# Forgetting attention: scores and running sums in two float32r products over all 128 rows

## What is computed

```python
log_f = jax.nn.log_sigmoid((f_logit + f_bias).astype(jnp.float32))
cum = jnp.transpose(jnp.cumsum(log_f, axis=1), (0, 2, 1))
scale = HEAD_DIM ** -0.5
outs = []
for i in range(s // FOX_BLOCK):                      # 4 blocks of 128 queries
    start, end = i * FOX_BLOCK, (i + 1) * FOX_BLOCK
    sc = jnp.einsum('bqhd,bkhd->bhqk', q[:, start:end], k[:, :end]) * scale
    sc = sc + cum[:, :, start:end, None] - cum[:, :, None, :end]
    causal = (start + jnp.arange(FOX_BLOCK))[:, None] >= jnp.arange(end)[None, :]
    sc = jnp.where(causal[None, None], sc, -jnp.inf)
    probs = jax.nn.softmax(sc, axis=-1).astype(v.dtype)
    outs.append(jnp.einsum('bhqk,bkhd->bqhd', probs, v[:, :end]))
out = jnp.concatenate(outs, axis=1).reshape(b, s, 1024) * jax.nn.silu(z)
```

## Time and profile before

| | |
|---|---|
| median of three runs | 3423.32 us (3422.49 to 3426.72) |
| span of the profiled execution | 3422.6 us |
| TensorE busy | 3340.3 us, 98% |
| GpSimd busy | 2116.8 us, 62% |
| VectorE busy | 1552.0 us, 45% |
| ScalarE busy | 878.8 us, 26% |

### The profile page before, as it was taken

One profiled execution on the slowest core, in us unless ns is written; L12 is line 12 of the kernel. 1 busy time (PEld: TensorE's weight loads), 2 busy tenths in 40 slices (PEclk: granted clock), 3 DMA queues, 4 the chain that ended last, 5 costly groups with the idle time before them and its releaser, 6 DMA issues.

```text
span 3422.6 us, 49035 instructions
## 1 busy us (share of the span) xinstructions
PE 3340.3 (98%) x16926; PEld 2712.7 (79%) x16926; DVE 1552.0 (45%) x2835; ACT 878.8 (26%) x1851; POOL 2116.8 (62%) x2084
## 2 busy tenths in 40 slices
PE   8999999999999999999999999999999999999997
PEld 6778788887777788887888778787878877788876
DVE  6544542106545541107674652333476656423325
ACT  2133211102133211103332540323132335313321
POOL 7745577767745577766557557454856566564455
PEclk9999999999999999999999999999999999999998
DMA  3212122222211222222222222112222222221111
GB/s 136 86 62 74 64 97 98 98 98 87 86 62 62 73 99 98 94 94 98 72 86 85 76 74 94 67 62 74 87 78 85 74 99 74 75 86 68 69 71 66
DMA packets 40030, 281.42 MB, mean 82 GB/s; under 512 B 4832, under 2 KB 5344, under 8 KB 6464
## 3 DMA queue, kind: packets, MB, share of 16 engines
q1 hardware_dynamic: 38880, 277.96, 22.8%
q10 hardware_dynamic: 992, 1.31, 0.1%
HBM read 277.16 MB, written 2.10 MB: 82 GB/s over the span
## 4 chain that ended last, share of the span: by engine, by line
PE 87%; DVE 7%; issue 3%; ACT 2%; POOL 1%; DMA 0%; DVEq 0%; ACTq 0%; SPq 0%; POOLq 0%
PE banks L380 21%; PE banks L382 20%; PE banks L381 20%; PE banks L639 2%; PE banks L640 2%; PE banks L641 2%; PE banks L423 2%; PE banks L424 2%; PE banks L425 2%; PE banks L915 1%; PE banks L939 1%; PE banks L926 1%; PE banks L610 1%; PE banks L918 1%; PE banks L857 1%
## 5 line engine op out<-in xcount | busy, mean ns | idle before, releaser
L343 POOL TENSOR_SCALAR whi<-raw 128x512 fp32r<-128x512 f32 x1040 | 725.9, 707 | 1271.5 <-PE banks L382 1037.4
L348 POOL TENSOR_TENSOR wlo<-raw,whi 128x512 fp32r<-128x512 f32 x1040 | 1435.7, 1391 | 0.0
L380 PE MATMUL banks<-xhi,whi 128*128 128x512 f32 x2832 | 1136.2, 401 | 30.4 <-POOL wlo L348 20.2
L382 PE MATMUL banks<-xhi,wlo 128*128 128x512 f32 x2832 | 1107.1, 391 | 0.0
L381 PE MATMUL banks<-xlo,whi 128*128 128x512 f32 x2832 | 1106.1, 391 | 0.0
L380 PEld LDWEIGHTS banks<-xhi,whi 128*128 128x128 f32 x2832 | 533.6, 188 | 163.7 <-issue 47.2
L381 PEld LDWEIGHTS banks<-xlo,whi 128*128 128x128 f32 x2832 | 533.9, 189 | 114.8 <-issue 8.2
L382 PEld LDWEIGHTS banks<-xhi,wlo 128*128 128x128 f32 x2832 | 533.2, 188 | 113.9
L380 PE MATMUL banks<-yhi,whi 128*128 128x512 f32 x544 | 214.7, 395 | 10.1 <-POOL wlo L348 5.2
L382 PE MATMUL banks<-yhi,wlo 128*128 128x512 f32 x544 | 211.8, 389 | 0.0
L381 PE MATMUL banks<-ylo,whi 128*128 128x512 f32 x544 | 211.8, 389 | 0.0
(11 more groups left out here) (277 smaller groups left out, 4197.6 us busy)
## 6 DMA issues: line engine op xcount, KB each, us to landing
raw<-weights SPq DMA_DIRECT2D x260, 1024.0 KB, 4.8
x<-x_in SPq DMA_DIRECT2D x4, 512.0 KB, 8.0
out<-merged SPq DMA_DIRECT2D x1, 2048.0 KB, 6.3
rot<-const SPq DMA_DIRECT2D x1, 512.0 KB, 11.7
rot<-const ACTq DMA_DIRECT2D x1, 512.0 KB, 3.7
wide_mask<-const ACTq DMA_DIRECT2D x1, 384.0 KB, 4.5
wide_mask<-const SPq DMA_DIRECT2D x1, 256.0 KB, 12.0
cst<-const SPq DMA_DIRECT2D x1, 232.0 KB, 9.3
```

Source lines behind the costliest of these rows:

```text
L343: pool.tensor_scalar(whi[p][:, w], raw[p][:, w], 1.0, 1.0, ALU.mult, ALU.mult).then_inc(s("hi_written"), 1)
L348: return pool.tensor_tensor(wlo[p][:, w], raw[p][:, w], whi[p][:, w].bitcast(F32), ALU.subtract)
L380: pe.matmul(dst, whi[p][:, w], hi[:, k, :], start=start and i == 0, stop=False)
L382: mm = pe.matmul(dst, wlo[p][:, w], hi[:, k, :], start=False, stop=stop and last_k)
```

## The change

The queries and keys of a pair of heads now come from one wave (q of the pair in one tile, k of the pair in the other), and are kept as four float32r tiles of 128 rows for each head h, `part[h]`, named by what they hold. With o the 64 rows of the head and z the other 64:

- Q_HL: rows o the high part of q, rows z its low part
- Q_HS: rows o the high part of q, rows z the selector column of the head, spread over 512 columns
- K_HH: the high part of k in both
- K_LC: rows o the low part of k, rows z the running sums

So Q_HL x K_HH + Q_HS x K_LC is high x high + low x high + high x low + the running sums. Two sets of these tiles alternate between pairs. ScalarE writes the high parts and the selectors (`pair_high`), VectorE the low parts (`pair_low`), in which it subtracts the high part from the PSUM bank; the sums are written to K_LC once a layer. `fox_pick` is no longer called in the loop. There are still 20 waves, in another order: the first pair and v of group 0 ahead of the loop, and two waves behind step 31. On ScalarE half_out moves behind the exponentials of the next step; on VectorE the work on a half wave (`half_low`) comes last in a step.

```diff
+def fox_kind(w):
+    g, i = divmod(w, 4)
+    if w >= 14:
+        return "gate", w - 14
+    return (("pair", 2 * g + 1), ("z", g), ("pair", 2 * g + 2), ("v", g + 1))[i]
...
-        fox_q = (sg[:, 0:4, :], q2)
-        fox_v = (sg[:, 4:6, :].rearrange("p a n -> p (a n)").rearrange("p (c n) -> p c n", c=QB), v2)
+        fox_pair = ((fox_even[:, 0], fox_even[:, 1]), (fox_odd0[:, :, :], fox_odd1[:, :, :]))
+        Q_HL, Q_HS, K_HH, K_LC = range(4)
+        fox_v = (v_even[:, :, :], v2[:, :, :])
...
-                wave_t(fox, 0, xhi, xlo, first_bank=0)
-                wave_t(fox + 1, 1, xhi, xlo, first_bank=4)
-                start_wave(fox + 2, 0)
-                wave_s_blocks(0, range(QB)).then_inc(wave_done, 1)
+                wave_t(fox, 0, xhi, xlo)
+                start_wave(fox + 1, 1)
+                wave_s_blocks(1, range(QB)).then_inc(wave_done, 1)
...
                 def fox_scores(k):
-                    g, m = divmod(k, PAIRS)
-                    if m == 0:
-                        pe.wait_ge(drained[1], fox + 4 * g + 4)
-                        pe.wait_ge(drained[0], fox + 4 * g + 4)
-                        pe.wait_ge(s("fox_ready"), L * GROUPS + g + 1)
+                    pair, i = divmod(k, QB)
+                    if i == 0:
+                        pe.wait_ge(s("fox_split"), 2 * (2 * GROUPS * L + pair + 1))
                     if k:
                         pe.wait_ge(s("fox_probs"), 2 * STEPS * L + 2 * k)
-                    r, i = fox_unit(2 * k)
                     w = (i + 1) * P
-                    q = fox_q[g % 2]
+                    part = fox_pair[pair % 2]
                     for h in range(2):
-                        o = 64 * h
-                        pe.matmul(psum[:, 4 + h, 0:w], q[o:o + 64, r // 2, i * P:w],
-                                  q[o:o + 64, 2 + r // 2, 0:w], start=True, stop=False)
-                    for h in range(2):
-                        pe.matmul(psum[:, 4 + h, 0:w], sel[:, r + h, :], cum[:, 1, 0:w],
+                        pe.matmul(psum[:, 4 + h, 0:w], part[h][:, Q_HL, i * P:w], part[h][:, K_HH, 0:w], start=True, stop=False)
+                        pe.matmul(psum[:, 4 + h, 0:w], part[h][:, Q_HS, i * P:w], part[h][:, K_LC, 0:w],
                                   start=False, stop=True).then_inc(s("fox_scores"), 1)
...
-                half_wave(4 * GROUPS, 0, False)
+                half_wave(4 * GROUPS, 0)
                 fox_output(STEPS - 1)
-                half_wave(4 * GROUPS, 1, False)
+                half_wave(4 * GROUPS, 1)
+                for half in range(2):
+                    half_wave(4 * GROUPS + 1, half)
...
+                def pair_high(pair, keys, src):
+                    part = fox_pair[pair % 2]
+                    if pair >= 2 and not keys:
+                        act.wait_ge(s("fox_scores"), 2 * STEPS * L + 8 * (pair - 1))
+                    own.begin()
+                    for h in range(2):
+                        o, z = slice(64 * h, 64 * h + 64), slice(64 - 64 * h, 128 - 64 * h)
+                        if keys:
+                            own(act.activation(part[h][o, K_HH, :], src[o, :], ACT.Copy))
+                            own(act.activation(part[h][z, K_HH, :], src[o, :], ACT.Copy))
+                        else:
+                            own(act.activation(part[h][o, Q_HL:Q_HS + 1, :], src[o, None, :].to_broadcast([64, 2, S]), ACT.Copy))
+                            c = C_SEL + 2 * pair + h
+                            own(act.activation(part[h][z, Q_HS, :], cst[z, c:c + 1].to_broadcast([64, S]), ACT.Copy))
+                    own.done()
+                    act.nop().then_inc(s("fox_high"), 1)
...
                 for k in range(STEPS):
                     g, m = divmod(k, PAIRS)
-                    half_out(fox_wave(g, m), m % 2)
                     fox_turned_out(2 * k)
                     fox_turned_out(2 * k + 1)
                     if k + 1 < STEPS:
                         fox_expo(2 * k + 2)
                         fox_expo(2 * k + 3)
+                    half_out(fox_wave(g, m), m % 2)
                     if m == 0 and g:
                         fox_y_hi(g - 1)
...
+                def pair_low(pair, keys, src, p):
+                    part = fox_pair[pair % 2]
+                    dve.wait_ge(s("fox_high"), 2 * (2 * GROUPS * L + pair) + keys + 1)
+                    own.begin()
+                    for h in range(2):
+                        o, z = slice(64 * h, 64 * h + 64), slice(64 - 64 * h, 128 - 64 * h)
+                        to, high = (part[h][o, K_LC, :], K_HH) if keys else (part[h][z, Q_HL, :], Q_HL)
+                        own(dve.tensor_tensor(to, src[o, :], part[h][o, high, :].bitcast(F32), ALU.subtract))
+                    own.done()
+                    dve.nop().then_inc(s("fox_split"), 1)
+                    dve.nop().then_inc(drained[p], 1)
...
-                fox_pick(0)
+                for part in fox_pair:
+                    for h, z in ((0, slice(64, 128)), (1, slice(0, 64))):
+                        own(dve.tensor_copy(part[h][z, K_LC, :], cum[0:64, 1, :].bitcast(F32)))
+                own.done()
+                pair_low(0, 0, bank(0), 0)
+                pair_low(0, 1, bank(1), 0)
...
-                    if m == PAIRS - 2 and g < GROUPS - 1:
-                        fox_pick(g + 1)
+                    half_low(fox_wave(g, m), m % 2)
```

More of the change, by code:

```diff
@@ L205, in program @@
         merged = sb("merged", [P, KT, S], F32, big)
+        over_sg = ExitStack()
+        fox_even = sb("fox_even", [P, 2, 4, S], F32R, over_sg)
+        over_sg.close()
         sg = sb("sg", [P, KT, S], F32, big)
@@ L225, in program @@
         second = ExitStack()
+        over_kv = ExitStack()
+        v_even = sb("v_even", [P, QB, 256], F32, over_kv)
+        over_kv.close()
         kv_first = sb("kv_first", [P, S], F32, second)
+        sel = sb("sel", [P, 4, P], F32R, second)
         cum = sb("cum", [P, 2, S], F32R, second)
-        sel = sb("sel", [P, 4, P], F32R, second)
         selp = sb("selp", [P, 2 * P], F32R, second)
@@ L243, in program @@
         t4 = ExitStack()
+        over_q2 = ExitStack()
+        fox_odd0 = sb("fox_odd0", [P, 4, S], F32R, over_q2)
+        over_q2.close()
         q2 = sb("q2", [P, 4, S], F32, t4)
@@ L250, in program @@
         st2 = sb("st2", [P, 4, 32], F32, t4)
+        over_q3 = ExitStack()
+        fox_odd1 = sb("fox_odd1", [P, 4, S], F32R, over_q3)
+        over_q3.close()
         q3 = sb("q3", [P, 3, S], F32, t4)
@@ L934, in fox_output @@
                         pe.wait_ge(s("fox_read"), L * GROUPS + g + 1)
-                        pe.wait_ge(drained[0], fox + 4 * g + 6)
+                        pe.wait_ge(drained[1], fox + 4 * g + 4)
                     pe.wait_ge(s("fox_pt"), 2 * STEPS * L + 2 * k + 2)
@@ L942, in fox_output, with half_wave @@
                     mm.then_inc(s("fox_outputs"), 1)
-                def half_wave(w, half, tokens):
-                    n, p = fox + 3 + w, (w + 1) % 2
+                def half_wave(w, half):
+                    n, p = fox + 2 + w, w % 2
                     if half == 0:
@@ L950, in half_wave @@
                     pe.wait_ge(drained[1 - p], n + p + half + 1)
-                    if tokens:
+                    if fox_kind(w)[0] == "v":
                         mm = wave_s_blocks(p, (2 * half, 2 * half + 1))
@@ L959, in _ @@
                     g, m = divmod(k, PAIRS)
-                    half_wave(fox_wave(g, m), m % 2, m >= 6 and g < GROUPS - 1)
+                    half_wave(fox_wave(g, m), m % 2)
                     fox_turn(2 * k)
@@ L1372, in _ @@
                 fox = base + W_FOX
[L1373 to L1377, removed]
+                def pair_high(pair, keys, src):
[14 more added lines that the diff above has]
+                    act.nop().then_inc(s("fox_high"), 1)
+                act.wait_ge(wave_done, fox + 1)
+                pair_high(0, False, bank(0))
+                pair_high(0, True, bank(1))
+                act.wait_ge(wave_done, fox + 2)
+                act.activation(fox_v[0], bank(2, 2).rearrange("p a (b n) -> p (a b) n", b=2), ACT.Copy).then_inc(drained[1], 2)
                 def fox_expo(u):
@@ L1396, in half_out @@
                 def half_out(w, half):
-                    n, p = fox + 3 + w, (w + 1) % 2
+                    n, p = fox + 2 + w, w % 2
                     if half == 0:
-                        act.wait_ge(s("first_half"), (4 * GROUPS + 1) * L + w + 1)
+                        act.wait_ge(s("first_half"), (4 * GROUPS + 2) * L + w + 1)
                     else:
@@ L1403, in half_out @@
                     src = bank(2 + half)
[L1404 to L1409, removed]
+                    kind, i = fox_kind(w)
+                    if kind == "z":
+                        act.activation(fox_y[i % 2][:, half, :], src, ACT.Tanh, scale=0.5).then_inc(s("fox_z"), 1)
+                    elif kind == "gate":
```

(41 more changed lines are left out.)

## The result

The changed kernel took 3400.26 us at the median of four runs (3396.90 to 3401.75) against 3422.90 us for the kernel before: ratio 0.9928, 95% interval 0.9915 to 0.9942, 22.6 us less. The forecast was 3396 us (3390 to 3409), faster. A second comparison, in which both kernels ran again, gave 0.9915 (0.9901 to 0.9928), some 29 us less.

What follows compares the result with a forecast made beforehand. TensorE was taken to bound the kernel; cheaper score products save 23.5 + 3.5 = 27.0 us, other work hidden. The span 3422.6 - 27.0 = 3395.6, with the median 0.7 above it, gave 3396 us, range 3390 to 3409.

Steps and rivals of the forecast that it cites:

- What bounds the kernel: Forgetting attention loop: TensorE busy 262.82 of 263.20 us, so its time counts in full, other engines' only if late.
- The price of the scores: Score products in the loop: 0.54, 0.68, 0.90, 1.12 us per step at 128 to 512 columns, saving 27.0 us.
- The bound by which each pair costs what L918 costs: Lower bound for the score products: four steps take 4.02 us, and the change saves 15 us.
- the narrowest: Score group of a 128-column step: 0.20 + 4 x 0.085 = 0.54 us, saving 0.25 us per step.
- Waves: 20 a layer before and after, one moved behind the loop at equal cost; exposed copy of first values stays 1.03 us.
- ScalarE and VectorE: Added copies (q half 3.2 us, k half 2.4) and subtractions (1.4 us a half) in the loop are hidden, costing nothing.
- The slack of 1.0 us: Margin before the half wave two steps on needs its drained bank, behind both q and k halves.
- Dearer handoffs: Rival on the score products: pairs cost what L918 costs, 15 us saved, 3408 us; chance 8%.
- the full gain: Rival on the score products: 32 us saved, 3391 us, needing 512 columns in 0.21 us; chance 8%.
- no effect: Rival: parts not taken as float32r, products pay as L915 does, no time saved, 3423 us or above; chance 3%.
- VectorE late: Rival: sharing with GpSimd stretches the subtractions to 1.54 us, 14 us given back, 3410 us; chance 7%.
- the fourth: Rival, slower than before: ScalarE's copies to the other 64 rows cost double, 34 us lost, 3429 us; chance 4%.

Runs made afterwards that it cites:

- run 2: The kernel before with the running sums (the L918 products) left out of the scores, nothing else changed; ratio 0.9941 against the kernel before.
- run 6: The changed kernel with the outputs of two steps taken together in every second step, using two more buffers for turned weights; 3395.62 us, ratio 0.9906 against the kernel before.
- run 7: As run 6, and ScalarE signals the high parts of q before it spreads the selectors; 3389.90 us, ratio 0.9888 against the kernel before.
- run 4: The changed kernel with ScalarE's order of before: half_out ahead of the turned weights and the next step's exponentials; 3408.16 us, ratio 0.9942 against the kernel before.
- Run 3: The changed kernel with the second score product of each head left out; 3385.55 us, ratio 0.9876 against the kernel before.
- run 5: The changed kernel with each of ScalarE's copies and selector spreads for a pair made twice; 3475.05 us, ratio 1.0136 against the kernel before.

## Why the prediction was right

**What bounds the kernel.** Right. TensorE's time counted in full: 26.7 us of rows went and 26.7 us of the loops.

**The price of the scores.** Right, 1.67 us in four steps for 1.72. The bound by which each pair costs what L918 costs fell: the second pair takes 0.22 to 0.47 us, where L918's took 0.37 to 0.66, since it carries no change of form (run 2). The term that was off is the narrowest, 0.59 us for 0.54: I had split L918's 0.37 into 0.20 and twice 0.085, and it is 0.15 and twice 0.11 (0.7 us in all). Run 2 shows the 0.20 us by itself, in front of a product of 512 columns. The Trainium skill's page "TensorEngine Tiling (Array Packing)", Key Properties, says that a switch of mode drains TensorE; the traces agree, in run 2 with 0.43 against 0.23 to 0.28 us, and in run 6, where 32 pairs of changes less gave 7.1 and, without the waits (run 7), 11.2 us.

**Waves.** Right: no wait came or went where the wave was moved, and the copy of the first values stayed at 1.03 us.

**ScalarE and VectorE.** Hidden, as forecast; copies 1.02, 0.63 and 0.59 us, subtractions 0.69. The slack of 1.0 us was wrong. The low part was done at 6.4 us for 6.2, with the bank wanted at 7.2, and the way from the last subtraction to TensorE's next product I counted at nothing. In run 4, where it lies on the chain, 0.20 us pass between the two (2205.33 to 2205.53), and the product then takes 0.50 us for 0.23. Run 3 puts the slack at some 0.1 us, and the waits of run 6 fit it. It took nothing from the result, but a reader who relies on the microsecond would make the next step, as run 6, 4 us dearer than it need be. The sentence that the move of half_out stands in front of nothing that TensorE awaits holds; that the move mattered was not said, and it is worth 7 us in the loops (run 4).

**The rivals.** Dearer handoffs, the full gain and no effect fell with the chain; VectorE late fell, at 0.69 us a subtraction; the fourth fell too, with copies at 0.59 to 1.02 us, undoubled. It priced copies of double length at 34 us; run 5, which doubled the work of both halves, showed its mechanism and 45 us; the price had counted on the slack of 1.0. Not among the rivals was what took most of the difference between 27.0 and 22.6 us: the clock outside the loops. The kernel before falls to 1.2 GHz in the same places, at some of them in each execution. The loss was 3.4 to 10.2 us in six profiles, so a forecast from one profile can be off by up to 7 us here, whatever the edit; the range, which had been drawn for the price of the scores, covered that by luck.

## What to carry to other kernels

Where TensorE is the bound, look in the chain at the first product behind each change of form, and count the changes: here a group of products cost its columns and 0.15 to 0.20 us for each, and work in the odd form is best gathered. A product that needs a few rows of its own can ride in the idle rows of one that is split in high and low parts. Work that is "hidden" should be given the time of its signals and of the next weight load, and be tested by shortening the step above it, since a miss costs the wait and, beyond it, the clock.

## What the runs showed of the hardware

Not expected: TensorE's granted clock fell from 2.4 to 1.2 GHz for 3.4 or 6.8 us behind idle stretches of 2.0 to 3.1 us, at about six places of the kernel, and at which of them varied between executions of the same kernel (losses 5.1 and 8.6 us for the kernel before): behind the same product it fell after 2.28 us in one execution and not after 2.34 in another. Waits of up to 2.9 us in a loop that is otherwise full brought falls of their own: five in a loop of 366 us, 11.9 us lost beside 23.8 us of waiting (run 5). A float32r product of 128 columns took 0.11 us in a row of such products, one of 256 took 0.12: below 256 columns hardly anything was saved, except for the first of a group behind the turns, 0.06.
